# Gather ring and weight places redealt (twelve and two for eleven and three), buffers laid out anew

## What is computed

```python
def peer(h, wq, subkeys, u_tab, v_tab):
    q = (t @ wq).reshape(-1, PEER_HEADS, 2, PEER_QDIM // 2)
    s = jnp.einsum('thpd,hpkd->thpk', q, subkeys).astype(jnp.float32)
    sv, si = lax.top_k(s, PEER_TOPK)
    cand = sv[:, :, 0, :, None] + sv[:, :, 1, None, :]
    cv, ci = lax.top_k(cand.reshape(..., PEER_TOPK * PEER_TOPK), PEER_TOPK)
    idx = i1 * PEER_KEYS + i2
    g = jax.nn.softmax(cv, axis=-1)
    ...
        act = jax.nn.gelu(jnp.einsum('td,thkd->thk', tb, u_tab[ib]))
        return jnp.einsum('thk,thkd->td', gb * act, v_tab[ib])
```

## Time and profile before

| | us |
|---|---|
| median of three runs | 2312.71 |
| lowest and highest of them | 2308.45, 2313.47 |
| the profiled execution, its own time | 2306.4 |
| its span, first to last instruction | 2304.6 |

### The profile page before, as it was taken

One profiled execution on the slowest core, in us unless ns is written; L12 is line 12 of the kernel. 1 busy time (PEld: TensorE's weight loads), 2 busy tenths in 40 slices (PEclk: granted clock), 3 DMA queues, 4 the chain that ended last, 5 costly groups with the idle time before them and its releaser, 6 DMA issues.

```text
span 2304.6 us, 23920 instructions
## 1 busy us (share of the span) xinstructions
PE 2060.9 (89%) x6960; PEld 1126.1 (49%) x6960; DVE 1597.9 (69%) x3904; ACT 953.3 (41%) x2795; POOL 997.0 (43%) x868
## 2 busy tenths in 40 slices
PE   8998998999998888988999998798799978888887
PEld 7785554555564444444554554346546423333222
DVE  3865778967766668888866667855686885666654
ACT  2024444543334444444454334533554443444433
POOL 0003444344444544444445445420344545455663
PEclk9999999999999999999999999999899999999999
DMA  9979999999999999999999999986799999999997
GB/s 405 426 296 388 426 420 427 427 426 427 426 427 426 427 426 426 427 426 427 419 426 427 427 427 427 426 314 284 306 425 426 426 427 426 428 426 427 427 427 319
DMA packets 133618, 943.22 MB, mean 409 GB/s; under 512 B 14832, under 2 KB 18544, under 8 KB 19568
## 3 DMA queue, kind: packets, MB, share of 16 engines
q0 software_dynamic: 110592, 805.36, 83.2%
q1 hardware_dynamic: 22896, 136.35, 14.2%
HBM read 940.60 MB, written 1.05 MB: 409 GB/s over the span
## 4 chain that ended last, share of the span: by engine, by line
PE 38%; DMA 34%; DVE 13%; issue 6%; POOL 5%; ACT 3%; SPq 0%; POOLq 0%; DVEq 0%; ACTq 0%
DMA uv<-uv_dram,stage_idx 32%; PE psum L1016 21%; PE psum L819 9%; DVE uv L1619 5%; POOL uv L1090 5%; PE psum L801 4%; PE psum L959 1%; DVE h L1321 1%; DMA uv<-in_dram 1%; DMA uv<-ada_dram 1%; ACT diag L1264 1%; PE psum L991 1%; PE psum L734 1%; ACT small L1260 1%; DVE work L1427 1%
## 5 line engine op out<-in xcount | busy, mean ns | idle before, releaser
L1016 PE MATMUL psum<-uv,diag 128*128 128x512 f32 x3072 | 1438.7, 611 | 185.1 <-ACT diag L1264 176.7
L1090 POOL DMA_INDIRECT uv<-uv_dram,stage_idx x768 | 965.2, 1257 | 1013.3 <-PE psum L1016 773.1
L1619 DVE CUSTOM_DVE_ANT_0 uv<-uv,h 128x1024 f32<-128x1024 f32 x768 | 932.8, 1225 | 521.6 <-DMA uv<-uv_dram,stage_idx 512.2
L1016 PEld LDWEIGHTS psum<-uv,diag 128*128 128x128 f32 x3072 | 567.1, 193 | 943.8 <-issue 522.8
L1258 ACT ACTIVATE small<-small 128x1 f32<-128x1 f32 x768 | 155.1, 202 | 1016.9 <-DVE small L1619 1015.8
L1264 ACT ACTIVATE diag<-const,small 128x128 f32<-128x128 f32 x768 | 308.4, 402 | 25.1
L819 PE MATMUL psum<-hT,wring 128*128 128x256 f32 (+1 forms) x1344 | 270.9, 355 | 0.0
L819 PEld LDWEIGHTS psum<-hT,wring 128*128 128x128 f32 x1344 | 233.5, 191 | 60.8 <-issue 36.4
L1260 ACT ACTIVATE small<-small,gw 128x1 f32<-128x1 f32 x768 | 226.2, 295 | 24.9
L1076 POOL COPY stage_idx<-idx 128x8 uint32<-128x8 uint32 x96 | 31.6, 329 | 264.2 <-DVE idx L1590 263.6
L1110 ACT ACTIVATE work<-psum 128x256 f32<-128x256 f32 (+2 forms) x127 | 48.3, 383 | 130.1 <-PE psum L819 100.6
(11 more groups left out here) (220 smaller groups left out, 1276.9 us busy)
## 6 DMA issues: line engine op xcount, KB each, us to landing
uv<-ada_dram SPq DMA_DIRECT2D x27, 1024.0 KB, 19.3
wring<-wq_dram SPq DMA_DIRECT2D x26, 1024.0 KB, 11.3
wring<-in_dram SPq DMA_DIRECT2D x23, 1024.0 KB, 9.1
uv<-uv_dram,stage_idx POOLq DMA_INDIRECT x768, 21.2
uv<-in_dram SPq DMA_DIRECT2D x11, 1024.0 KB, 23.2
uv<-ada_t_dram SPq DMA_DIRECT2D x10, 1024.0 KB, 25.8
wring<-ada_dram SPq DMA_DIRECT2D x9, 1024.0 KB, 23.0
uv<-out_w_dram SPq DMA_DIRECT2D x4, 1024.0 KB, 21.0
```

The source lines that it names most:

```text
L1016: last = mm(acc[:, b, :], diag[:, s % DIAGS, :], uv[:, s % RING, D + 512 * b:D + 512 * (b + 1)], start=(c == 0), stop=(c == NSEL - 1))
L1090: nc.gpsimd.indirect_dma_start(out=uv[:, r, :], out_offset=None, in_=tables[stage // 2], in_offset=bass.IndirectOffsetOnAxis(ap=places[:, ...
L1619: v.tensor_tensor_reduce(out=uv[:, r, 0:D], in0=uv[:, r, 0:D], in1=h2[:, row_of[stage], t, :], scale=1.0, scalar=0.0, op0=ALU.mult, op1=AL ...
```

## The change

The ring has twelve places in place of eleven and `wring` two in place of three, so the two together still hold fourteen blocks of 8 KB per partition. `LAST_SLOTS` moves by one place with them. In stage 0 the second tile's part of head 1 is done ahead of head 2 (it stood behind it), which frees the first two `wq` blocks earlier; in stage 2 the attention's last projection stands ahead of head 2's query (it stood behind it). The tensors are declared in another order, so that the ring, `wring`, the activations and the gates follow each other at distances that are multiples of 1024 bytes; the first of them, the ring, begins at byte 2176 of a partition. It began at byte 93440. One small tensor is dropped (`ms_heads` is now `ss_heads`). What is computed and the 122 blocks are the same.

```diff
-WRING = 3
+WRING = 2
...
-LAST_SLOTS = (5, 6, 7, 8, 9, 10)
+LAST_SLOTS = (6, 7, 8, 9, 10, 11)
...
-RING = 11
+RING = 12
...
-    return [(first, first + 5, rms(stage, two) + norm(stage, 1)[1:] + [("turn_back", stage, 1)] + query(stage, 0, two)
-             + score(stage, 0, two)),
-            (first + 5, first + 14, query(stage, 2) + score(stage, 2, one) + find(stage, 2, one) + score(stage, 2, two)),
-            (first + 14, first + 24, query(stage, 1, two) + score(stage, 1, two) + query(stage, 3) + score(stage, 3, one) + find(stage, 3, one)
-             + score(stage, 3, two)),
-            (first + 24, 39, query(stage, 4) + score(stage, 4) + query(stage, 5))]
+    return [(first, first + 8, rms(stage, two) + norm(stage, 1)[1:] + [("turn_back", stage, 1)] + query(stage, 0, two)
+             + score(stage, 0, two) + query(stage, 1, two) + score(stage, 1, two)),
+            (first + 8, first + 16, query(stage, 2) + score(stage, 2, one) + find(stage, 2, one) + score(stage, 2, two)),
+            (first + 16, first + 26, query(stage, 3) + score(stage, 3, one) + find(stage, 3, one) + score(stage, 3, two)),
+            (first + 26, 39, query(stage, 4) + score(stage, 4) + query(stage, 5))]
...
-    out = [(6, 10, query(stage, 2, one) + score(stage, 2, one)), (11, 20, find(stage, 2, one)),
+    out = [(14, 17, query(stage, 2, one) + score(stage, 2, one)), (17, 23, find(stage, 2, one)),
...
-             (8, 11, [("o_norm", 2, 1, 0, HEADS)]), (11, 13, [("o_turn", 2, 1, 0, HEADS)]), (1, 7, find(2, 1, one)),
-             (14, 20, out_t[1])]
+             (6, 8, [("o_norm", 2, 1, 0, HEADS)]), (8, 9, [("o_turn", 2, 1, 0, HEADS)]), (1, 7, find(2, 1, one)),
+             (9, 13, out_t[1])]
...
+        uv = sb("uv", [P, RING, 2 * D])
+        wring = sb("wring", [P, WRING, BLK_W])
+        x = sb("x", [P, 2 * TT, D])
+        h2 = sb("h2", [P, 2, TT, D])
+        hT = sb("hT", [P, KC, TOK])
+        work = sb("work", [P, 8704])
...
-        ss_heads, ms_heads = (sb(s, [P, 16]) for s in ("ss_heads", "ms_heads"))
-        root_heads = ms_heads
+        ss_heads = ms_heads = root_heads = sb("ss_heads", [P, 16])
```

More of the change, by code:

```diff
@@ L404, in sem @@
             return ctx.enter_context(nc.semaphore(name))
+        uv = sb("uv", [P, RING, 2 * D])
[4 more added lines that the diff above has]
+        work = sb("work", [P, 8704])
+        vx = sb("vx", [P, TT, MIX])
+        wst = sb("wst", [P, 8 * P])
+        gate_mix = sb("gate_mix", [P, D])
+        gate_peer = sb("gate_peer", [P, D])
+        keys = sb("keys", [P, 2, SUB_W])
+        diag = sb("diag", [P, DIAGS, P])
         const = sb("const", [P, W_CONST])
-        wst = sb("wst", [P, 8 * P])
         ones = sb("ones", [P, P])
-        x = sb("x", [P, 2 * TT, D])
         silu_c = sb("silu_c", [P, KC, QW])
@@ L414, in build @@
         modg = sb("modg", [P, 3, KC])
[L415 to L420, removed]
         small = sb("small", [P, 9 * 2 + 3 * HEADS + 3 * RING + 8])
@@ L426, in build @@
         unused = small[:, 30 + 3 * RING:38 + 3 * RING]
-        ss_heads, ms_heads = (sb(s, [P, 16]) for s in ("ss_heads", "ms_heads"))
-        root_heads = ms_heads
+        ss_heads = ms_heads = root_heads = sb("ss_heads", [P, 16])
         smax, nmax, psums = (sb(s, [P, 2, 2]) for s in ("smax", "nmax", "psums"))
         prec = sb("prec", [P, TT * HEADS, 2])
-        uv = sb("uv", [P, RING, 2 * D])
-        diag = sb("diag", [P, DIAGS, P])
         idx = sb("idx", [P, TT, NSEL], U32)
@@ L437, in build @@
         stage_idx = sb("stage_idx", [P, GROUPS, GROUP], U32)
-        work = sb("work", [P, 8704])
         def view(base, off, *shape):
@@ L475, in build @@
         kxT = view(h2_0, 1024, HEADS, TOK)
-        vx = sb("vx", [P, TT, MIX])
         qk = view(work, 0, TT, MIX)
```

## The result

| | us |
|---|---|
| kernel before, median of 4 runs | 2310.58 |
| changed kernel, median of 4 runs | 2335.66 (2334.23 to 2336.21) |
| ratio, 95% interval | 1.0107, 1.009 to 1.0125 |
| profiled execution of the changed kernel, own time and span | 2336.21, 2334.4 |

A forecast was written before the change was run, and what follows sets the result against it. The prediction took the kernel to be bound by its transfers, 943.22 MB at 427 GB/s. Its terms, -3.0 for the opening and 0 for all else, gave a median of 2309.7 us, with a range of 2303 to 2319.

The forecast's parts named there:

- What bounds the kernel, and where a loss can lie: Whole kernel: bound by transfers at 427 GB/s; an edit counts only through low-share stretches or bytes, which stay the same.
- rival 4: All packets written 128 above a multiple of 256 slow by 1.6%: +34 us, 2347 us; chance 0.04.
- The layout, taken as 0: All buffers 128 above a multiple of 256: taken as free because offsets 0 and 192 cost the same per MB; 0.
- The opening, -3.0 (bounds 0 and 4.5): At 185 to 200 us, behind slot 0's start: of 4.5 us lost to a dry queue, 3.0 come back.
- a sign of being wrong: Indices' chain ahead of slot 0 or 512 changes length, or share falls below 0.98 in slot stretches at 1.01.
- The twelfth slot elsewhere, 0 with a bound of 1: Long windows outside the opening: no share left for a deeper ring to win; 0, up to 1 us for small dips.
- Later first wq block, 0: Before 137 us: queue may be dry 2.5 us, hidden by the low window at 150 to 165 us; 0.
- Head 2's block and indices, 0: Stage 0: block issued near 214 us, indices at 251 to 254.5, covered by the queue; 0, bound 5.
- rival 3: Head 2's late indices starve the gathers if its search ends past 259.6 us: +6, 2318.7 us; chance 0.15.
- Stage 2's order, 0: Stage 2: head 2's search comes some 12 us later, with the same queue cover; 0.
- rival 1: Whole opening loss and small dips come back, queue never dry: -5 to -7, 2306.7 us at -6; chance 0.24.

The follow-up runs named there:

- m1: Load-only kernel, 1 MB blocks at starts 0 to 256 bytes: 427 or 428 GB/s on multiples of 256, 420 to 422 off; one block in eight off lost nothing.
- m2: Load-only kernel with mixtures, sources off and smaller pieces: every second block off 428 GB/s, eight in a row 425; 4096-byte pieces 421 aligned, 409 off.
- e2: Kernel before with ss_heads and ms_heads declared behind the ring, which then begins 128 above a multiple of 256: 2340.27 us, ratio 1.0128.
- e3: Kernel before with only ms_heads declared behind the ring, which then begins 192 above a multiple of 256: 2340.42 us, ratio 1.0127.
- e1: Changed kernel with 128 bytes of small tensors declared ahead of the ring, which then begins on a multiple of 256: 2306.07 us, 0.9974 of the kernel before.
- e4: Kernel before, its orders and counts kept, with the aligned declarations of e1: ratio 1.0003 to the kernel before.
- e5: e1 with eleven slots, three weight places and LAST_SLOTS 5 to 10, so new orders without new counts: ratio 1.0002 to the kernel before.
- e8: Kernel before with the output projection's third block in ring place 6 and fourth in 7, formerly the other way round: 2306.54 us, ratio 0.9992.
- e7: e1 run again beside later runs on one chip: ratio 0.9982 to the kernel before.
- e10: e1 with ada blocks from the 44th on in ring places alone, so the first wq block goes early; projection blocks as in e9: 2303.82 us, ratio 0.9977.
- e9: e1 with LAST_SLOTS 5 to 10, so that place 7 holds the projection's third block: 2305.22 us, ratio 0.9979 to the kernel before.

## Why the prediction was wrong, point by point

1. *What bounds the kernel, and where a loss can lie:* right. The long windows were at share 1.01 before and after; neither a wait nor a lost slot explains the 25 us, and the range failed on the one edit that touches the rate of a full queue. The sign that the prediction had named for rival 4, 420 GB/s at 200 to 1500 us, is the one that came.
2. *The layout, taken as 0: this is the step that failed.* It read from the earlier trace rows that loads at 192 above a multiple of 256 cost as much per MB as the gathers on one. The row is true (though its digits, 5.5 in a hundred, leave room for 1.3% and not only 0.4%), and the conclusion was not: those loads are 5 in 100 of the bytes, single blocks among aligned gathers, and m1 and m2 show that such blocks ride free (one in eight, even every second), while an unbroken stream pays 4 to 5 ns a packet. The packet records of 1000 to 1500 us show it on the very same weight places, at 192 in all three kernels: in the kernel before their packets took 309.0 ns in the mean (the gathers 309.9), in e2 and e3, with the ring off, 314.3 and 313.3 (the gathers 314.7 and 314.9). A stray block says nothing of a stream. e3 puts the ring at the same 192 and pays 1.27%.
3. *Rival 4* had the mechanism, with +34 us. Measured: +29.6 between e1 and the changed kernel, +29.0 and +29.1 in e2 and e3 (2311.28 beside them). Most of the difference to 34 is the size of the cost: the rate fell from 426 to 420, 1.4% and not 1.6%, which is 31 us of 2209 as an estimate. That the rest is hidden where TensorE's chain decides (ahead of slot 0 and in the gap) is argued and not shown. Its chance of 0.04 rested on step 2 alone.
4. *The opening, -3.0 (bounds 0 and 4.5):* the mechanism held in its parts: the waiting gather expected at 184.9, found at 185.90, with the first gather 2.3 us later than in the earlier trace rows. That is a longer indices' chain ahead of slot 0, which the prediction had named as a sign of being wrong; in e4, e5 and e8, whose order ahead of slot 0 is the old one, the first gather is 1.4 to 1.8 us late too, with the lower clock, so most of it is not the change's. Slot 0's dot product expected 5.75 us behind its issue, found 6.0; TensorE's idle time expected 0.8, found 1.19; the share at 185 to 190 us 0.92. Between e4 and e7 or e1 the opening is worth 2.0 to 2.5 us, a little less than even the 2.4 that was called sure in one of the two, and within the bounds.
5. *The twelfth slot elsewhere, 0 with a bound of 1:* mis-sized. It is 0.6 to 1.7 us, at 1115 to 1130 us, a dip that a window of 1300 us does not show. The share of 1.01 over 1300 us was taken for no loss anywhere, though its rate of 426 for 427 left 3 us open.
6. *Later first wq block, 0:* e10 against e9, 1.4 us in the medians and no difference that the intervals can tell. *Head 2's block and indices, 0:* the block was issued at 212.86 (expected 214), the indices were there at 249.64 (expected 251 to 254.5, whose upper end leaves out the head start: with it the sum ends at 252.2), and the share at 250 to 270 us is 1.02, so rival 3's starving did not happen. *Stage 2's order, 0:* e5.

Without the offset the forecast of -3.0 would have met -4.3 to -5.2 us (the medians of e7 and e1 against the kernel before; by their ratios' intervals -2 to -6 and -4 to -8). That lies between the forecast and rival 1 (-5 to -7), and so does the queue: at 185 to 190 us its share is 0.88 in e7, and 1.01 in e1, where it does not run dry at all. The parts that were found, 2.0 to 2.5 and 0.6 to 1.7 us, add up to 2.6 to 4.2; the remainder is not placed. Whether the wait in step 4 or the slot in step 5 depends on the number of weight places was not tried alone.

## What to carry to other kernels

When declarations move, look up the byte of the partition at which each large DMA target begins, and keep the one that takes most of the stream on a multiple of 256; here 128 bytes were 29.6 us of 2336, against 4 to 5 us for all the rest of the change. Don't price a property of a saturated stream by a few transfers that have it among many that don't, and read a rate in narrow windows before calling it full. Where one edit changes both the rate and the waits, separate them by the rate at full DMA share first.

## What the runs showed of the hardware

- The cost of a start off a multiple of 256 bytes in SBUF is per packet: 4.5 to 4.7 ns for 1024 to 4096 bytes at an offset of 128 (m2), 4 to 6 ns for 8192 bytes at all offsets of 32 to 224 (309 to between 313 and 315 ns in m1). It is there only after 4 to 6 MB off in a row; a source off by 32 or 128 bytes costs nothing that shows (426 GB/s in m2).
- Pieces of 4096, 2048 and 1024 bytes, all aligned and 256 bytes apart in SBUF, move at 421, 409 and 386 GB/s (m2) where 8192 move at 427 (m1).
- TensorE's granted clock at 127 to 138 us was 0.84 in the changed kernel, e1 and e4 to e9, and 1.00 in e10, e2, e3 and the kernel before, though TensorE's work there is the same in all of them; 32 products took 8.7 to 8.9 us at 0.84 and 7.17 at 1.00, and the first gather came at 167.9 to 168.8 us and at 166.1 to 167.1. Each is one execution, and what decides it is open.
